# A sixth pair of k tiles by the 2x2 recurrence in the SwiGLU mixer, with three wide buffers for the weights' high parts served in turn

## Chip, core and metric

The kernel runs on one core of one Trainium2 chip. The metric is the device time of one execution in microseconds, lower is better. Every product is made in three passes on TensorE (high by high, high by low, low by high) from float32 values split into an fp32r high part and an fp32r rest.

## What is computed

Two layers over 256 positions of width 2048: a mixer (a gated recurrence beside a gated MLP in layer 0, windowed attention in layer 1), then in each layer the dense SwiGLU mixer, which the change touches:

```
def swiglu(h, w_in, w_out):
    g, u = jnp.split(h @ w_in, 2, axis=-1)        # w_in: 2048 x (2 x 5632)
    return (jax.nn.silu(g) * u) @ w_out           # w_out: 5632 x 2048
...
x = x + swiglu(rms_norm(x, ffn_norm[layer]), w_ffn_in[layer], w_ffn_out[layer])
```

## The kernel before

**Blocks and groups.** The 5632 hidden columns are cut into 11 blocks of 512. Block 0 goes through an older path of 16 chunks (lines 902 and 464 split their weights, line 1498 multiplies); each chunk counts up chunk_used. Blocks 1 to 10 go through groups, 12 a block and the same list each time: eight groups for the gate and up projections of block f (N_UP = 8, GROUPS_UP), then four down groups, D0 to D3, that multiply the hidden block f-1 into the four column groups of the output. A group is 1 MB of weights: 128 partitions by 4 slots of 512 columns. A group of kind plain holds one pair of k tiles and takes 24 matmuls, as a down group does. A group of kind strassen holds a pair of k tiles that is multiplied by a 2x2 scheme with seven products, 21 matmuls; it needs three sums of its slots (w_sum) and their high and low parts too. Before, a block is: plain 5, strassen 0, 1, 2, plain 6, strassen 3, 4, plain 7, D0, D1, D2, D3. Below, g0 to g11 are the places in this list (g8 to g11 are D0 to D3).

**Who does what for a group.** SP loads it into group_raw[g % 6] when the group six places earlier is used (line 353). VectorE, for a strassen group, makes three sums (sum_group: lines 1230, 1234, 1236). ScalarE casts the four slots to the high part group_hi[g % 4] (hi_group: line 708 for strassen, 715 else) and for strassen the three sums (line 711). VectorE subtracts to get the low parts (lo_group: line 1248, and 1253 for the sums). TensorE waits for group_lo_ready, multiplies (line 1714) and counts up group_used. Every engine takes its work strictly in the order in which its program lists it.

**Buffers of the high parts.** group_hi has four places, taken as g % 4: the cast of group g waits until group g-4 is used (free_group, line 699), and so does VectorE's second sum of a strassen group, which writes w_sum[g % 4] (line 1233). In a layer's first block the first four groups wait for chunks of block 0 instead (line 697): none for g0 and g3, 12 and 15 for g1 and g2.

**The results.** The gate and up sums of a block stand in eight banks of PSUM; out_sums and out_parts (lines 1268 to 1281) bring them together on VectorE after g9 and g10, silu and hidden (lines 677, 1167) make the hidden block, and turn_blocks (line 1177) with two DMAs on GpSimd's queue turns it, after which rows_hi and rows_lo (lines 683, 1183) split it. D0 and D2 write banks 0 and 1, D1 and D3 banks 2 and 3. ScalarE copies each out as y0 to y3 (copy_y, line 732), and GpSimd's queue adds it to x by a DMA (line 423). ScalarE's order in block f+1 for the four copies of block f is:

```
hi_(0)
if not first:
    copy_y(before, layer, 0)
    copy_y(before, layer, 1)
hi_(1)
if not first:
    copy_y(before, layer, 2)
hi_(2)
if not first:
    copy_y(before, layer, 3)
```

TensorE starts D2 of a block only when that block's y0 is copied and D3 when y1 is (line 1779), and g1 of the next block when y3 is (line 1772). In the last block the four copies stand after the block, with no cast of a following block ahead of the first.

**VectorE's order in a block** is g0 to g4, rows_lo, g5 to g9, out_sums, g10, out_parts, g11, hidden, turn_blocks; in the first block rows_lo comes after g5, and hidden and turn_blocks of block 0 stand between g1 and g2.

Of the kernel before, what the change touches and what calls it, by code (L numbers as in the profile page):

```python
# [20 lines left out]
F32R = mybir.dt.float32r  # L21
# [5 lines left out]
P = 128  # L27
# [4 lines left out]
W = 512  # L32
# [23 lines left out]
RING = 8  # L56
# [18 lines left out]


BLOCKS = FB - 1
GROUPS_UP = [("plain", 5), ("strassen", 0), ("strassen", 1), ("strassen", 2),
             ("plain", 6), ("strassen", 3), ("strassen", 4), ("plain", 7)]
N_UP = len(GROUPS_UP)  # L80
BLOCK_GROUPS = N_UP + GROUPS
LAST_STRASSEN = max(g for g, (kind, _) in enumerate(GROUPS_UP) if kind == "strassen")
HI_DONE = list(itertools.accumulate([2 if kind == "strassen" else 1 for kind, _ in GROUPS_UP] + [1] * GROUPS))
PAIRS = sum(kind == "strassen" for kind, _ in GROUPS_UP)
STRASSEN_BEFORE = [sum(kind == "strassen" for kind, _ in GROUPS_UP[:g]) for g in range(N_UP)]


# [18 lines left out]
def trunk(nc, x_in, final_norm, w_ab_in, a_lb_raw, b_v_norm, w_ab_out, w_qkv, c_sinks, w_c_out,  # L106
# [4 lines left out]
    with ctx:  # L111
# [9 lines left out]
        def sem(name):  # L121
# [14 lines left out]
        scratch = bias_at + 8 * KB  # L136
        place[0] = scratch + 76 * KB
        u_mid = sb("u_mid", [P, W])
        consts = sb("consts", [P, N_CONST, P])
        junk = sb("junk", [P, W])  # L140
        cols = sb("cols", [P, 80])
# [42 lines left out]
        gate = sb("gate", [P, NT, 1024], at=r1 + 36 * KB)  # L184
        end = r1 + 44 * KB

        group_hi = [sb("g0_hi", [P, 4, W], F32R, at=bias_at), sb("g1_hi", [P, 7, W], F32R, at=hi_at),
                    sb("g2_hi", [P, 7, W], F32R, at=hi_at + 14 * KB), sb("g3_hi", [P, 7, W], F32R, at=bias_at + 8 * KB)]
        raw_places = [raw_at, raw_at + 8 * KB] + [lo_at + 8 * KB * i for i in range(4)]
        group_raw = [sb(f"g{i}_raw", [P, 4, W], at=place_) for i, place_ in enumerate(raw_places)]  # L190
        group_lo = [sb(f"g{i}_lo", [P, 4, W], F32R, at=place_) for i, place_ in enumerate(raw_places)]
# [1 line left out]
        sum_lo = [None] + [sb(f"w{i}_lo", [P, 3, W], F32R, at=bias_at + (16 + 6 * i) * KB) for i in range(1, 4)]  # L193
        s_size = 512 * PAIRS
        s_hi = [sb(f"s{i}_hi", [P, PAIRS, P], F32R, at=bias_at + 40 * KB + i * s_size) for i in range(4)]
        s_lo = [sb(f"s{i}_lo", [P, PAIRS, P], F32R, at=bias_at + 50 * KB + i * s_size) for i in range(4)]
        s_sum = sb("s_sum", [P, 4, PAIRS, P], at=bias_at + 60 * KB)
        x_sum = sb("x_sum", [P, PAIRS, 2, T], at=bias_at + 22 * KB)
        gu = sb("gu", [P, 4, W], at=bias_at + 68 * KB)
# [258 lines left out]
        def _(act):  # L458
# [234 lines left out]

            def free_group(f, layer, g, first, base):

                if first and g < 4:
                    act.wait_ge(chunk_used, RING * base + (0, 12, 15, 0)[g])
                else:
                    act.wait_ge(group_used, f * BLOCK_GROUPS + (group_at(layer, 0) + g - 3))

            def hi_group(f, layer, g, first, base):

                free_group(f, layer, g, first, base)
                src, dst = group_raw[g % 6], group_hi[g % 4]
                if g < N_UP and GROUPS_UP[g][0] == "strassen":
                    n = 3 * (STRASSEN_BEFORE[g] - PAIRS)
                    act.wait_ge(sum_step, f * (3 * PAIRS) + (layer * BLOCKS * 3 * PAIRS + n + 1))
                    act.copy(dst[:, 0:4, :].rearrange("p s w -> p (s w)"),  # L708
                             src[:, :, :].rearrange("p s w -> p (s w)")).then_inc(group_hi_ready, 1)
                    act.wait_ge(sum_step, f * (3 * PAIRS) + (layer * BLOCKS * 3 * PAIRS + n + 3))  # L710
                    act.copy(dst[:, 4:7, :].rearrange("p s w -> p (s w)"),  # L711
                             w_sum[g % 4][:, :, :].rearrange("p s w -> p (s w)")).then_inc(group_hi_ready, 1)
                else:
                    act.wait_ge(pair_landed[g % 6], f * 64 + (32 * (group_at(layer, 0) // 6 + g // 6 + 1)))
                    act.copy(dst[:, 0:4, :].rearrange("p s w -> p (s w)"),  # L715
                             src[:, :, :].rearrange("p s w -> p (s w)")).then_inc(group_hi_ready, 1)
# [17 lines left out]
            def ffn(layer, base):  # L734

                root(2 * layer + 1)
                act.wait_ge(rstd_ready, 2 * layer + 2)
                ahead(base + 1, 2)
                for n, i in enumerate((0, 2, 1, 3)):
                    act.wait_ge(s_step, 5 * layer + n + 2)  # L740
                    act.copy(s_hi[i][:, :, :], s_sum[:, i, :, :]).then_inc(s_hi_ready, 1)
                ahead(base + 1, 5)
                silu(0, layer, base)
                ahead(base + 1, 7)

                def block(f, first):

                    def hi_(g):
                        hi_group(f, layer, g, first, base)

                    before = 0 if isinstance(f, int) and f == 2 else f - 2
# [10 lines that stand above are left out]
                    hi_(3)  # L762
                    hi_(4)
                    if not first:
                        rows_hi(f - 1, layer, hT[0][0])
                    hi_(5)
                    if first:
                        rows_hi(f - 1, layer, hT[0][0])
                    for g in range(6, 10):
                        hi_(g)  # L770
                    copy_p1(f, layer)
                    hi_(10)
                    hi_(11)
                    silu(f, layer, base)

                block(1, True)
                block(2, False)
                with act.Fori(3, FB - 1) as f:
                    block(f, False)
                block(FB - 1, False)  # L780
                copy_y(FB - 2, layer, 0)
                copy_y(FB - 2, layer, 1)
                last = base + FFN_ROUNDS - 1
                act.wait_ge(group_used, group_at(layer, FB - 1) + 10)
                his(last, 0, 3)
                copy_y(FB - 2, layer, 2)
                hT_his(FB - 1, layer, hT[1][0])
                act.wait_ge(group_used, group_at(layer, FB - 1) + 11)
                his(last, 3, 6)
                copy_y(FB - 2, layer, 3)  # L790
                done[0] = last * RING + 6
# [106 lines left out]
        def _(dve):  # L898
# [324 lines left out]

            def sum_group(f, layer, g, first):

                b, w = group_raw[g % 6], w_sum[g % 4]
                n = 3 * (STRASSEN_BEFORE[g] - PAIRS)
                step = f * (3 * PAIRS) + (layer * BLOCKS * 3 * PAIRS + n)
                dve.wait_ge(pair_landed[g % 6], f * 64 + (32 * (group_at(layer, 0) // 6 + g // 6 + 1)))
                dve.tensor_tensor(b[:, 1, :], b[:, 1, :], b[:, 0, :], ALU.subtract).then_inc(sum_step, 1)  # L1230
                dve.wait_ge(sum_step, step + 1)
                if not first or g >= 4:
                    dve.wait_ge(group_used, f * BLOCK_GROUPS + (group_at(layer, 0) + g - 3))
                dve.tensor_tensor(w[:, 0, :], b[:, 3, :], b[:, 1, :], ALU.subtract).then_inc(sum_step, 1)
                dve.wait_ge(sum_step, step + 2)
                dve.tensor_tensor(w[:, 1:3, :], b[:, 0:4:2, :], w[:, 0:1, :].broadcast_to([P, 2, W]),  # L1236
                                  ALU.subtract).then_inc(sum_step, 1)

            def lo_group(f, layer, g):

                src, hi_part, lo_part = group_raw[g % 6], group_hi[g % 4], group_lo[g % 6]
                strassen = g < N_UP and GROUPS_UP[g][0] == "strassen"
                ready = f * HI_DONE[-1] + ((layer * BLOCKS - 1) * HI_DONE[-1] + HI_DONE[g])
                dve.wait_ge(group_hi_ready, ready - 1 if strassen else ready)
# [5 lines left out]
                                        hi_part[:, 0:4, :].rearrange("p s w -> p (s w)"), ALU.subtract)  # L1250
                if strassen:
                    dve.wait_ge(group_hi_ready, ready)
                    ins = dve.tensor_tensor(sum_lo[g % 4][:, :, :].rearrange("p s w -> p (s w)"),  # L1253
                                            w_sum[g % 4][:, :, :].rearrange("p s w -> p (s w)"),
                                            hi_part[:, 4:7, :].rearrange("p s w -> p (s w)"), ALU.subtract)
                ins.then_inc(group_lo_ready, 1)

# [26 lines left out]
            def ffn(layer, base):  # L1284
# [6 lines left out]
                ahead(base + 1, 7)  # L1291
                group(1, layer, 0, True)
                group(1, layer, 1, True)
                hidden(0, layer, base)
                turn_blocks(0, layer)
                group(1, layer, 2, True)

                def block(f, first, last):
                    for g in range(3 if first else 0, 5):
# [190 lines left out]
        def _(pe):  # L1490
# [227 lines left out]

            def plain_group(g, first, last):

                hi_part, lo_part = group_hi[g % 4], group_lo[g % 6]
                for q in range(4):
                    k = 2 * GROUPS_UP[g][1] + q // 2
                    for t in range(NT):
# [5 lines left out]

            def strassen_group(g, first, last):

                hi_part, lo_part, sums_lo = group_hi[g % 4], group_lo[g % 6], sum_lo[g % 4]
                p = GROUPS_UP[g][1]
                t0, t1 = slice(0, P), slice(P, T)
                x_part = lambda k, ts: (xT_hi[:, k, ts], xT_lo[:, k, ts])
# [8 lines left out]

            def down_group(g):

                hi_part, lo_part = group_hi[g % 4], group_lo[g % 6]
                n = g - N_UP
                for k in range(4):  # L1750
                    for t in range(NT):
# [190 lines left out]
def group_at(layer, f):  # L1942

    return (layer * BLOCKS + f - 1) * BLOCK_GROUPS
# [38 lines left out]
```

## Time and profile before

| | us |
|---|---|
| median of 3 runs | 2034.26 (2033.28 to 2034.81) |
| the profiled execution | 2033.34 |
| its span | 2031.5 |

The grouped blocks run from about 458 to 1081 us in layer 0 and from about 1378 to 2001 us in layer 1, that is some 1245 us of the span. Engines: PE is TensorE's matmul, PEld its weight load, DVE VectorE, ACT ScalarE, POOL GpSimd, SP SyncE. A timeline's columns are start, duration, engine, line, operation and tiles, and in brackets the engine's idle time before the instruction and who ended it. Matmuls overlap, so their pace is read from start to start, not from their durations.

### The profile page before, as it was taken

The page shows a single profiled execution, that of the slowest core. Times are in us where ns is not written, and L with a number is a line of the kernel's source. Part 1 is how long each engine was busy: PE and PEld are TensorE (multiplying, and loading weights), DVE is VectorE, ACT ScalarE, POOL GpSimd, SP SyncE. Part 2 cuts the span into 40 slices and gives each one's busy share as a digit, 9 for nine tenths or more (in the row PEclk, how much of TensorE's full clock was granted, in tenths as well). Part 3 has the DMA queues.
Part 4 walks back from the last instruction along what each step waited for, and adds up shares of the span by engine and source line. Part 5 has one row for each costly group of instructions (what it writes and reads, how often), then busy time and mean ns, then how long its engine had stood idle before and what let it go on. Part 6 is the DMA issues. An engine that isn't in the chain of part 4 may idle for free.

```text
span 2031.5 us, 24678 instructions
## 1 busy us (share of the span) xinstructions
PE 2008.3 (99%) x9278; PEld 1666.2 (82%) x9278; DVE 1647.5 (81%) x1556; ACT 1179.9 (58%) x1195; POOL 170.6 (8%) x216
## 2 busy tenths in 40 slices
PE   8999999999999999999999999999999999999998
PEld 6888888887888888888888887787888888888886
DVE  5656777779999999999986467779999999999995
ACT  6745655555665555656556466555656556655554
POOL 0000000100111101111100000100111101111010
PEclk9999999999999999999999999999999999999999
DMA  7755443866998888988877644666988889988885
GB/s 262 228 177 166 159 151 131 275 208 209 269 256 253 243 248 261 268 248 256 244 244 228 190 145 145 218 222 222 269 248 251 246 248 268 267 251 238 249 261 160
DMA packets 237187, 461.40 MB, mean 227 GB/s; under 512 B 16480, under 2 KB 21376, under 8 KB 236992
## 3 DMA queue, kind: packets, MB, share of 16 engines
q1 hardware_dynamic: 202832, 386.97, 56.6%
q0 software_dynamic: 30496, 69.22, 16.8%
q10 hardware_dynamic: 3792, 4.34, 0.7%
q8 instruction: 39, 0.64, 0.1%
q14 instruction: 28, 0.23, 0.0%
HBM read 401.10 MB, written 17.29 MB: 206 GB/s over the span
## 4 chain that ended last, share of the span: by engine, by line
PE 92%; DVE 4%; ACT 2%; DMA 1%; issue 1%; ACTq 0%; SPq 0%; DVEq 0%
PE ps L1714 58%; PE ps L1498 30%; DVE g_lo L1248 1%; PE ps L1605 1%; DVE w_lo L902 1%; DMA raw<-in_w_ab_in 1%; DVE w_sum L1236 0%; DVE w_lo L1253 0%; PE ps L1524 0%; PE ps L1865 0%; ACT w_hi L464 0%; PE ps L1840 0%; ACT probs L830 0%; ACT junk L507 0%; DMA x<-in_x 0%
## 5 line engine op out<-in xcount | busy, mean ns | idle before, releaser
L1248 DVE TENSOR_TENSOR g_lo<-g_raw,g_hi 128x2048 fp32r<-128x2048 f32 x240 | 547.3, 2288 | 54.2 <-ACT g_hi L715 30.9
L902 DVE TENSOR_TENSOR w_lo<-raw,w_hi 128x1024 fp32r<-128x1024 f32 x248 | 294.4, 1220 | 153.8 <-ACT w_hi L464 145.4
L715 ACT CAST g_hi<-g_raw 128x2048 fp32r<-128x2048 f32 x140 | 265.5, 1911 | 156.1 <-PE ps L1714 150.4
L464 ACT ACTIVATE w_hi<-raw 128x1024 fp32r<-128x1024 f32 x248 | 254.0, 1056 | 140.2 <-DMA raw<-in_w_ab_in 50.1
L708 ACT CAST g_hi<-g_raw 128x2048 fp32r<-128x2048 f32 x100 | 191.5, 1915 | 221.0 <-DVE g_raw L1230 221.0
L1714 PE MATMUL ps<-g_hi,xT_hi 128*128 128x512 f32 x780 | 303.9, 390 | 5.0 <-DVE w_lo L1253 5.0
L1714 PE MATMUL ps<-g_hi,xT_lo 128*128 128x512 f32 x780 | 303.4, 389 | 0.0
L1498 PE MATMUL ps<-w_hi,xT_hi 128*128 128x512 f32 x672 | 265.3, 395 | 1.2 <-DVE xT_lo L921 1.1
L1714 PE MATMUL ps<-g_lo,xT_hi 128*128 128x512 f32 x680 | 264.6, 389 | 0.0
L1498 PE MATMUL ps<-w_hi,xT_lo 128*128 128x512 f32 x672 | 262.3, 390 | 0.0
L1498 PE MATMUL ps<-w_lo,xT_hi 128*128 128x512 f32 x672 | 262.1, 390 | 0.0
L1714 PE MATMUL ps<-g_hi,h0T_hi 128*128 128x512 f32 x640 | 249.1, 389 | 0.0
L1714 PE MATMUL ps<-g_hi,h0T_lo 128*128 128x512 f32 x640 | 249.0, 389 | 0.0
L1714 PE MATMUL ps<-g_lo,h0T_hi 128*128 128x512 f32 x640 | 249.0, 389 | 0.0
L423 POOL DMA_DIRECT2D x<-y x80 | 95.9, 1198 | 990.2 <-ACT y L732 704.2
L1714 PEld LDWEIGHTS ps<-g_hi,xT_hi 128*128 128x128 f32 x780 | 146.4, 188 | 37.0 <-DVE w_lo L1253 6.7
L1253 DVE TENSOR_TENSOR w_lo<-w_sum,g_hi 128x1536 fp32r<-128x1536 f32 x100 | 175.1, 1751 | 0.0
L1714 PEld LDWEIGHTS ps<-g_hi,xT_lo 128*128 128x128 f32 x780 | 146.4, 188 | 30.4
L1714 PE MATMUL ps<-g_hi,s_hi 128*128 128x512 f32 x400 | 155.7, 389 | 0.0
L1714 PE MATMUL ps<-g_hi,s_lo 128*128 128x512 f32 x400 | 155.6, 389 | 0.0
L711 ACT CAST g_hi<-w_sum 128x1536 fp32r<-128x1536 f32 x100 | 148.5, 1485 | 11.1 <-DVE w_sum L1236 10.1
L1498 PEld LDWEIGHTS ps<-w_hi,xT_hi 128*128 128x128 f32 x672 | 126.6, 188 | 28.5 <-DVE xT_lo L921 1.5
(222 smaller groups left out, 3041.1 us busy)
## 6 DMA issues: line engine op xcount, KB each, us to landing
g_raw<-in_w_ffn_in SPq DMA_DIRECT2D x320, 512.0 KB, 4.8
g_raw<-in_w_ffn_out SPq DMA_DIRECT2D x160, 512.0 KB, 4.7
raw<-in_w_ab_in SPq DMA_DIRECT2D x96, 512.0 KB, 4.8
x<-y POOLq DMA_DIRECT2D x80, 512.0 KB, 6.6
raw<-in_w_qkv SPq DMA_DIRECT2D x40, 512.0 KB, 4.5
raw<-in_w_ab_out SPq DMA_DIRECT2D x32, 512.0 KB, 4.7
raw<-in_w_ffn_in SPq DMA_DIRECT2D x32, 512.0 KB, 4.6
raw<-in_w_c_out SPq DMA_DIRECT2D x32, 512.0 KB, 5.2
```

Source lines behind the costliest of these rows:

```text
L423: pool.dma_start(x[:, :, n * W:(n + 1) * W], y[n % 2][:, :, :], accum_op=ALU.add).then_inc(y_landed[n % 2], 16)
L464: act.activation(w_hi[:, s, :], raw[:, s % RAWS, :], ACT.Copy).then_inc(hi_ready, 1)
L708: act.copy(dst[:, 0:4, :].rearrange("p s w -> p (s w)"), src[:, :, :].rearrange("p s w -> p (s w)")).then_inc(group_hi_ready, 1)
L711: act.copy(dst[:, 4:7, :].rearrange("p s w -> p (s w)"), w_sum[g % 4][:, :, :].rearrange("p s w -> p (s w)")).then_inc(group_hi_ready, 1)
L715: act.copy(dst[:, 0:4, :].rearrange("p s w -> p (s w)"), src[:, :, :].rearrange("p s w -> p (s w)")).then_inc(group_hi_ready, 1)
L902: dve.tensor_tensor(w_lo[:, s, :], raw[:, s % RAWS, :], w_hi[:, s, :], ALU.subtract).then_inc(lo_ready, 1)
L1248: ins = dve.tensor_tensor(lo_part[:, 0:4, :].rearrange("p s w -> p (s w)"), src[:, :, :].rearrange("p s w -> p (s w)"), hi_part[:, 0:4, :] ...
L1253: ins = dve.tensor_tensor(sum_lo[g % 4][:, :, :].rearrange("p s w -> p (s w)"), w_sum[g % 4][:, :, :].rearrange("p s w -> p (s w)"), hi_pa ...
L1498: ins = pe.matmul(banks[:, t, :], a[:, k0 + h, ts], w[:, s, h * W:(h + 1) * W], start=first and h == 0 and i == 0, stop=last and h == 1 an ...
L1605: ins = pe.matmul(side[t][:, c], E[:, t, c], E[:, t, c], start=True, stop=True)
L1714: ins = pe.matmul(bank, a, w, start=first and i == 0, stop=last and i == 2)
```

## The change

GROUPS_UP becomes plain 6, strassen 0 to 5, plain 7: k tiles 10 and 11, which were plain 5, are multiplied as the sixth strassen pair, and the six strassen groups g1 to g6 stand in a row. There are still 12 groups and 1 MB for each. The places of the high parts are taken from a list, HI_OF, in which place 0 (four slots, no room for sums) serves g7 and g10 and the three wide places 1, 2 and 3 serve the others. HI_BACK tells how many groups back the same place was used last: 3, 5, 3, 3, 3, 3, 3, 9, 4, 3, 3, 6 for g0 to g11, where it was 4 for all. The high places 1 and 2 exchange their addresses, s_lo moves partly over the masks in consts, and in the last block three casts wait for one group more. In a layer's first block the three sums of g2 stand ahead of hidden of block 0 on VectorE.

```
-GROUPS_UP = [("plain", 5), ("strassen", 0), ("strassen", 1), ("strassen", 2),
-             ("plain", 6), ("strassen", 3), ("strassen", 4), ("plain", 7)]
+GROUPS_UP = [("plain", 6)] + [("strassen", p) for p in range(6)] + [("plain", 7)]
...
+HI_OF = [2, 3, 1, 2, 3, 1, 2, 0, 3, 2, 0, 1]
+HI_BACK = [next(d for d in range(1, BLOCK_GROUPS + 1) if HI_OF[(g - d) % BLOCK_GROUPS] == h) for g, h in enumerate(HI_OF)]
...
-        group_hi = [sb("g0_hi", [P, 4, W], F32R, at=bias_at), sb("g1_hi", [P, 7, W], F32R, at=hi_at),
-                    sb("g2_hi", [P, 7, W], F32R, at=hi_at + 14 * KB), sb("g3_hi", [P, 7, W], F32R, at=bias_at + 8 * KB)]
+        group_hi = [sb("g0_hi", [P, 4, W], F32R, at=bias_at), sb("g1_hi", [P, 7, W], F32R, at=hi_at + 14 * KB),
+                    sb("g2_hi", [P, 7, W], F32R, at=hi_at), sb("g3_hi", [P, 7, W], F32R, at=bias_at + 8 * KB)]
...
-        s_lo = [sb(f"s{i}_lo", [P, PAIRS, P], F32R, at=bias_at + 50 * KB + i * s_size) for i in range(4)]
+        s_lo_at = [bias_at + 52 * KB, bias_at + 55 * KB, consts_at + 512, consts_at + 512 + s_size]
+        s_lo = [sb(f"s{i}_lo", [P, PAIRS, P], F32R, at=s_lo_at[i]) for i in range(4)]
...
             def free_group(f, layer, g, first, base):
-                if first and g < 4:
-                    act.wait_ge(chunk_used, RING * base + (0, 12, 15, 0)[g])
+                if first and g < HI_BACK[g]:
+                    act.wait_ge(chunk_used, RING * base + (0, 15, 12, 0)[HI_OF[g]])
                 else:
-                    act.wait_ge(group_used, f * BLOCK_GROUPS + (group_at(layer, 0) + g - 3))
+                    act.wait_ge(group_used, f * BLOCK_GROUPS + (group_at(layer, 0) + g + 1 - HI_BACK[g]))
             def hi_group(f, layer, g, first, base):
...
-                src, dst = group_raw[g % 6], group_hi[g % 4]
+                src, dst = group_raw[g % 6], group_hi[HI_OF[g]]
...
-                act.wait_ge(group_used, group_at(layer, FB - 1) + 11)
+                act.wait_ge(group_used, group_at(layer, FB - 1) + 12)
                 his(last, 3, 6)
...
             def sum_group(f, layer, g, first):
...
-                if not first or g >= 4:
-                    dve.wait_ge(group_used, f * BLOCK_GROUPS + (group_at(layer, 0) + g - 3))
+                if not first or g >= HI_BACK[g]:
+                    dve.wait_ge(group_used, f * BLOCK_GROUPS + (group_at(layer, 0) + g + 1 - HI_BACK[g]))
...
                 group(1, layer, 0, True)
                 group(1, layer, 1, True)
+                sum_group(1, layer, 2, True)
                 hidden(0, layer, base)
                 turn_blocks(0, layer)
-                group(1, layer, 2, True)
+                lo_group(1, layer, 2)
```

## Rows read from the trace of the kernel before

**Rows 1.** The page: span, and busy time of each engine.
```profile
span 2031.5 us, 24678 instructions
PE 2008.3 (99%) x9278; PEld 1666.2 (82%) x9278; DVE 1647.5 (81%) x1556; ACT 1179.9 (58%) x1195; POOL 170.6 (8%) x216
```
**Rows 2.** TensorE's waits over the span: us in total, times, longest.
```profile
PE ps L1714 <- DVE w_lo L1253: 5.0, 4, 1.4
```
**Rows 3.** Windows: a middle block (D3's end to the next), then layer 0's first block.
```profile
832.90:894.80 61.90, 61.90 (x274) 51.26 (x273) 56.73 (x43) 36.53 (x26) 7.62 (x9) 1.00 0.85 255
458.40:523.50 65.10, 62.56 (x275) 51.17 (x274) 62.43 (x50) 38.29 (x26) 7.48 (x11) 1.00 0.72 225
```
**Rows 4.** VectorE's waits within the middle block, 832.9 to 894.8 us.
```profile
DVE g_lo L1248 <- ACT g_hi L715: 1.2, 1, 1.2
DVE u_mid L1268 <- ACT gu L722: 1.1, 1, 1.1
```
**Rows 5.** Timeline of TensorE: a stall of the first block, then D3's last matmul.
```profile
489.43 0.39 PE L1714 MATMUL ps<-g_hi,s_lo 128*128 128x512 f32 x1
491.20 0.50 PE L1714 MATMUL ps<-g_hi,xT_hi 128*128 128x512 f32 x1 [1.38 <-DVE w_lo L1253]
491.54 0.39 PE L1714 MATMUL ps<-g_lo,xT_hi 128*128 128x512 f32 x1
...
832.48 0.39 PE L1714 MATMUL ps<-g_hi,h0T_lo 128*128 128x512 f32 x1
832.71 0.39 PE L1714 MATMUL ps<-g_hi,xT_hi 128*128 128x512 f32 x1
```
**Rows 6.** Timeline of VectorE in a middle block, g1 to g5.
```profile
824.98 2.29 DVE L1248 TENSOR_TENSOR g_lo<-g_raw,g_hi 128x2048 fp32r<-128x2048 f32 x1 [0.99 <-ACT g_hi L708]
...
835.63 0.68 DVE L1230 TENSOR_TENSOR g_raw<-g_raw 128x512 f32<-128x512 f32 x1
...
838.42 2.29 DVE L1248 TENSOR_TENSOR g_lo<-g_raw,g_hi 128x2048 fp32r<-128x2048 f32 x1
...
842.30 2.28 DVE L1248 TENSOR_TENSOR g_lo<-g_raw,g_hi 128x2048 fp32r<-128x2048 f32 x1
844.50 1.22 DVE L1183 TENSOR_TENSOR h0T_lo<-hid_rows,h0T_hi 128x1024 fp32r<-128x1024 f32 x1
845.64 0.68 DVE L1230 TENSOR_TENSOR g_raw<-g_raw 128x512 f32<-128x512 f32 x1
```
**Rows 7.** Timeline of ScalarE at the start of a middle block: cast of g0, then y0, y1, y3.
```profile
816.66 1.91 ACT L715 CAST g_hi<-g_raw 128x2048 fp32r<-128x2048 f32 x1 [2.36 <-PE ps L1714]
818.48 1.00 ACT L732 COPY y<-ps 128x1024 f32<-128x1024 f32 x1
822.03 1.02 ACT L732 COPY y<-ps 128x1024 f32<-128x1024 f32 x1 [2.54 <-PE ps L1714]
...
833.77 1.02 ACT L732 COPY y<-ps 128x1024 f32<-128x1024 f32 x1 [0.54 <-DMA x<-y]
```
**Rows 8.** Timelines of ScalarE and of VectorE at layer 0's entry into the first block.
```profile
444.74 1.91 ACT L715 CAST g_hi<-g_raw 128x2048 fp32r<-128x2048 f32 x1 [3.05 <-DMA g_raw<-in_w_ffn_in]
...
446.68 2.29 DVE L1248 TENSOR_TENSOR g_lo<-g_raw,g_hi 128x2048 fp32r<-128x2048 f32 x1 [3.74 <-ACT g_hi L715]
...
458.48 1.41 DVE L1167 SCALAR_TENSOR_TENSOR hid<-ps,rstd,hid 128x512 f32<-128x512 f32 x2 [2.86 <-PE ps L1498]
...
463.89 2.29 DVE L1248 TENSOR_TENSOR g_lo<-g_raw,g_hi 128x2048 fp32r<-128x2048 f32 x1
```
**Rows 9.** Timeline of GpSimd's queue: the DMA that adds y1.
```profile
824.99 1.18 POOL L423 DMA_DIRECT2D x<-y  x1 [3.35 <-issue]
```
**Rows 10.** Timeline of TensorE's first wait and of early matmuls.
```profile
7.08 1.94 PE L1524 MATMUL ps<-consts,x 128*128 128x128 f32 x8 [7.08 <-DMA x<-in_x]
...
12.37 0.63 PE L1498 MATMUL ps<-w_hi,xT_lo 128*128 128x512 f32 x1
12.80 0.63 PE L1498 MATMUL ps<-w_hi,xT_hi 128*128 128x512 f32 x1
```

More of the change, by code:

```diff
@@ L138, in trunk @@
         u_mid = sb("u_mid", [P, W])
+        consts_at = place[0]
         consts = sb("consts", [P, N_CONST, P])
@@ L711, in hi_group @@
                     act.copy(dst[:, 4:7, :].rearrange("p s w -> p (s w)"),
-                             w_sum[g % 4][:, :, :].rearrange("p s w -> p (s w)")).then_inc(group_hi_ready, 1)
+                             w_sum[HI_OF[g]][:, :, :].rearrange("p s w -> p (s w)")).then_inc(group_hi_ready, 1)
                 else:
@@ L1224, in sum_group @@
             def sum_group(f, layer, g, first):
-                b, w = group_raw[g % 6], w_sum[g % 4]
+                b, w = group_raw[g % 6], w_sum[HI_OF[g]]
                 n = 3 * (STRASSEN_BEFORE[g] - PAIRS)
@@ L1239, in lo_group @@
             def lo_group(f, layer, g):
-                src, hi_part, lo_part = group_raw[g % 6], group_hi[g % 4], group_lo[g % 6]
+                src, hi_part, lo_part = group_raw[g % 6], group_hi[HI_OF[g]], group_lo[g % 6]
                 strassen = g < N_UP and GROUPS_UP[g][0] == "strassen"
@@ L1252, in lo_group @@
                     dve.wait_ge(group_hi_ready, ready)
-                    ins = dve.tensor_tensor(sum_lo[g % 4][:, :, :].rearrange("p s w -> p (s w)"),
-                                            w_sum[g % 4][:, :, :].rearrange("p s w -> p (s w)"),
+                    ins = dve.tensor_tensor(sum_lo[HI_OF[g]][:, :, :].rearrange("p s w -> p (s w)"),
+                                            w_sum[HI_OF[g]][:, :, :].rearrange("p s w -> p (s w)"),
                                             hi_part[:, 4:7, :].rearrange("p s w -> p (s w)"), ALU.subtract)
@@ L1719, in plain_group @@
             def plain_group(g, first, last):
-                hi_part, lo_part = group_hi[g % 4], group_lo[g % 6]
+                hi_part, lo_part = group_hi[HI_OF[g]], group_lo[g % 6]
                 for q in range(4):
@@ L1731, in strassen_group @@
             def strassen_group(g, first, last):
-                hi_part, lo_part, sums_lo = group_hi[g % 4], group_lo[g % 6], sum_lo[g % 4]
+                hi_part, lo_part, sums_lo = group_hi[HI_OF[g]], group_lo[g % 6], sum_lo[HI_OF[g]]
                 p = GROUPS_UP[g][1]
@@ L1746, in down_group @@
             def down_group(g):
-                hi_part, lo_part = group_hi[g % 4], group_lo[g % 6]
+                hi_part, lo_part = group_hi[HI_OF[g]], group_lo[g % 6]
                 n = g - N_UP
```

## The prediction

> **What bounds the kernel now.** I read the page first. TensorE is busy 2008.3 of 2031.5 us [rows 1], and over the whole span it waited for VectorE in the groups four times, 5.0 us in all [rows 2]. So TensorE sets the time. But busy shares are an average, and the change works in the grouped blocks alone, so the windows come next [rows 3]: a middle block takes 61.9 us, all of it TensorE's, and VectorE is busy 56.73 us of it, far more than its 81% of the page. In a layer's first block TensorE already has 2.5 us idle (65.10 less 62.56). The reader is to see that there are two engines near the bound.
>
> TensorE's pace: two neighbouring matmuls start at 832.48 and 832.71, 0.23 us apart [rows 5]; to another digit, a middle block has 273 matmuls (3 plain x 24, 5 strassen x 21, 4 down x 24) in 61.9 us, 0.2267 us each. So a strassen group is 4.76 us, any other 5.44.
>
> VectorE's pace, from start to start [rows 6]: a strassen group 835.63 to 842.30, 6.67 us; a plain or down group 842.30 to 844.50, 2.20; rows_lo 844.50 to 845.64, 1.14. The sums of a strassen group are 2.79 of its 6.67 (835.63 to 838.42).
>
> **The sum if only TensorE counted.** One pair turns from 24 to 21 matmuls in 20 blocks: 60 x 0.2267 = 13.6 us less. The block would be 61.2 us.
>
> **VectorE.** A group of 2.20 us becomes one of 6.67, so 4.47 us more a block. How much room is there? Of the 61.9 us it waits 1.2 and 1.1 us [rows 4] and 0.52 and 0.99 at g1; of these the 0.99 is for ScalarE's cast and not for TensorE [rows 6]. Its work with the small gaps between instructions is thus 61.9 - 3.8 = 58.1 us; with 4.47 it is 62.6, and 63.6 if the 0.99 stays. That is above 61.2. But it is an average as well, and the order in the block matters more: six strassen groups in a row take VectorE 6 x 6.67 = 40.0 us and TensorE 28.6, so VectorE loses 11.4 us of lead there (before: runs of three and two). How much lead it can have is set by when a place of high parts comes free.
>
> **The chain through D3.** g2 now takes a place last used by g11, that is D3, three back. So VectorE's second sum of g2 can't start before D3 is used, as a sum of g1 is held now. Call the start of g0's first matmul after D3 zero. An engine released by a group's end starts 0.2 us after that point (D3 ends at 832.71, two groups of 5.44 earlier D1 ended, 821.83, and y1 started at 822.03) [rows 5, 7]. From there: g2 needs two sums and its low parts, 6.67 less the first sum's 0.8, which is done already: it is ready for TensorE at 6.1. g3 and g4 at 12.8 and 19.4, rows_lo 20.6, g5 27.2, g6 33.9. Do the casts hold it longer? Their places are free in time: g3's at 5.44, g4's at 10.2, g5's at 15.0, each before VectorE comes to it. TensorE would like to start g6 at 5.44 + 5 x 4.76 = 29.2. It waits first at g5 (2.7 us behind, and 2.0 more at g6), and g6 starts at 33.9 + 0.06 wake-up. A matmul after a stall has its successor 0.34 us later and not 0.23 (491.20, 491.54), 0.11 more [rows 5]. g6 starts 4.8 us later than TensorE could. Then g6, g7 and the downs: 4.76 + 5 x 5.44 = 32.0.
>
> **The copy of y0.** g0 took the place of D0 before (four back, g8); now it takes that of D1 (three back, g9). ScalarE's order is hi_(0), then y0. Before, the cast of g0 started 0.27 us after D0's end (816.66 against 832.71 - 3 x 5.44 = 816.39), y0 started at 818.48 and was copied at 819.48, while TensorE was still in D1 until 821.83: hidden [rows 5, 7]. Now the same cast starts 0.27 us after D1's end, and D2 needs y0 copied. So TensorE stands between D1 and D2 for 0.27 + 1.82 + 1.02 + 0.06 = 3.17 us, with the 0.11 after a stall 3.28. Nothing covers it: D2 is next in TensorE's order. This happens in nine blocks of a layer (in the tenth no cast stands ahead of y0): 18 x 3.28 = 59 us.
>
> **A middle block then:** 33.9 + 0.17 + 32.0 + 3.28 = 69.4 us against 61.9, 7.5 more. Eight of them a layer: 60.0.
>
> **The last block** has the chain and no wait for y0: 66.1 against 61.9, 4.2 more (what else it does is as before). Its casts of three chunks wait for all 12 groups instead of 11; three chunks of TensorE, 12 x 0.2267 = 2.7 us each, stand before they are used, 8.2 us for a cast and a subtraction of some 2.3: nothing. y3 is copied behind these casts, some 3 us later, and is needed by TensorE only after four chunks, 10.9 us: nothing.
>
> **The first block.** The high part of g0 sits in place 2, and waits for 12 chunks of the block before. The 16th ends at 458.48 as VectorE sees it, so the 12th at 458.48 - 4 x 2.72 = 447.6, while g0's cast started at 444.74 before [rows 8]. VectorE starts g0 at 447.6 + 1.94 = 449.5 (was 446.68), has g0 and g1 at 458.4, the moved sums of g2 at 461.2, and hidden and turn_blocks (458.48 to the sums of g2, where the rest of 463.89 - 458.48 = 5.4 less 2.74 is 2.7) at 463.9. The low part of g2 starts at 463.9, where it started before: the moved sums give 2.7 us and the late g0 takes them. Hidden is done at 462.6, before TensorE ends g0 at 463.7. Then g3, g4, g5 by 6.67, rows_lo, g6: 463.9 + 3.9 + 20.0 + 1.1 + 6.7 = 495.6, so TensorE starts g6 at 495.7 where it was 491.20 [rows 5, 8]. With the wait for y0: 4.6 + 3.3 = 7.9 us more.
>
> **Small things.** The sums of the positions before block 0 grow by a fifth; VectorE waits 3.74 us ahead of g0 there [rows 8] and more now, so I take 0, with 2 us a layer as the bound if they delay a chunk instead. Loads: 1 MB a group as before, six places, and the block is longer: 0, and a DMA share of 0.85 [rows 3] that falls. GpSimd's queue: y1 was copied at 823.05, its DMA issued at 824.99, and y3's copy waited for it until 833.77, 10.7 us after the copy [rows 7, 9]. y1 is now copied about 10.1 us before zero, so y3 can go at 0.6, while ScalarE comes to it at 3.6 (behind the two casts of g2), ready at 4.6, before g1 at 5.44: 0. Should it be later, up to 2.7 us of it vanish in the wait at g5.
>
> **Sum.** A layer: 7.9 + 60.0 + 4.2 = 72.1, two layers 144. The profiled execution took 2033.3, so 2177.5, and 0.9 us of difference to the median shown gives 2178. I forecast 2178 us, 7.1% slower.
>
> **The rivals.**
> *TensorE's work decides* (faster, 2020.7 us). For it: TensorE waits 5 us in all. It holds if VectorE's work stays under 61.2 us and y0 is copied in time. The point where it decides is 61.2 - 58.1 = 3.1 us of added work, and the work added is 4.47. 3 in 100.
> *VectorE decides, but only by its total*: 63.6 a block, 1.7 x 20 = 34, the first blocks' g6 some 3 us more each beyond that: 2074 us. It needs places that come free early enough, against the threes of HI_BACK. 3 in 100.
> *No wait for y0*, as where the copy were issued ahead of the cast; the chain through D3 alone: 2178 - 59 = 2119 us. The order of ScalarE's program speaks against it. 3 in 100.
> *The chain through D3 is covered*, since the sums of g2 to g6 find slack that I missed; y0's wait alone: 2034 - 13.6 + 59 + 10.6 for g6 of the two first blocks (4.6 late and 0.7 not saved, each) = 2090 us. Against it: the chain has only work of VectorE itself in it, at the pace of rows 6. 3 in 100.
> *TensorE's clock falls in the stalls.* The granted clock is 1.00 in both windows of rows 3, over the stall of 1.38 us too, where the next matmuls came at 0.23 again. Only at the start, after 7.08 us without work, the pace was 0.43 (12.37 to 12.80) [rows 10], the lower of the two levels; some eight matmuls ran so, from 10.07 us on, 1.6 us lost. After each stall of 3.2 us that would be 18 x 1.6 = 29 us: 2207; with those at g5 and g6 in part, up to 2235. Against it: the stall is half of the one at the start, and TensorE is full before it. 9 in 100. The Trainium skill has a rule that speaks for this rival: TensorE: Matmul & The Clock Gate, section "Why this matters for your kernels", asks to avoid idle gaps of TensorE between bursts of matmuls, or the clock falls back to half. By that rule the result would be nearer 2207 us than 2178; no stall as long as these is in the middle of this trace.
> *A DMA is late too*: y1's landing behind the rows of the hidden block, some 1 to 2 us a block, 2195 to 2215. For it: y3 waited 0.54 us for it already [rows 7]. Against: the 2.7 us at g5 that swallow it. 3 in 100.
>
> The forecast has 76 in 100. Its own uncertainty is half a microsecond a block in either direction, 2166 to 2190. The four cases below it hold 12 in 100 and lie far off, so the range goes down only to 2155, room for slack of a microsecond a block that I have not seen; above it takes in the clock's first price and most of the late DMA, 2212, and leaves out the clock's higher ones. A change under 0.2% is about what a measurement of this kernel can't tell from none. Faster 0.03, within 0.2% 0.01, slower 0.96.
>
> **What would show it.** The window of a middle block: 69.4 us, TensorE busy about 61 to 62, VectorE about 61. TensorE's waits: y (ScalarE, line 732) 18 times, near 3 us each; w_lo some 4 to 5 us a block, at g5 and g6. ScalarE's y0 no longer idle before D1's end. VectorE's second sum of g2 waiting for TensorE, some 2 us. ScalarE's cast of g0 in the first block at 447.6, and TensorE's start of g6 near 495.7. The granted clock 1.00 throughout. The forecast is wrong if D2 follows D1 without a gap, if VectorE is not waiting ahead of g2, or if the clock of the blocks is below 1.

## The result and the profile after

The changed kernel takes 2204.01 us (2202.75 to 2205.66, 4 runs) against 2034.1 us: a ratio of 1.0837, 95% interval 1.0823 to 1.0851, 170 us slower. The forecast was 2178 us in a range of 2155 to 2212.

The page of the changed kernel, its first lines, the granted clock by slices, and the chain by engine:

```profile
span 2203.9 us, 24482 instructions
PE 2054.6 (93%) x9218; PEld 1677.8 (76%) x9218; DVE 1735.0 (79%) x1636; ACT 1211.5 (55%) x1215; POOL 170.5 (8%) x216
...
PEclk9999999999999999999999999999999999999999
...
PE 62%; DVE 26%; issue 6%; ACT 4%; DMA 1%; ACTq 0%; DVEq 0%; SPq 0%
```

Against [rows 1], TensorE has its 60 matmuls less (9218), and it is idle for 149.3 us of the span where it was idle for 23.2. That is 126 us more; the other 46 us are busy time, slower matmuls among it. The two largest of its waits over the span, where [rows 2] had 5.0 us:

```profile
PE ps L1718 <- DVE w_lo L1256: 76.1, 34, 2.8
PE ps L1718 <- ACT y L735: 54.5, 18, 3.1
```

Both are the waits that were forecast: y0 in 18 blocks, and the row of strassen groups. Two middle blocks, D3's end to the next (start:end, length, busy time and count of PE, PEld, DVE, ACT, POOL, then the granted clock, DMA share, GB/s), to hold against the first of [rows 3]:

```profile
534.50:604.20 69.70, 62.19 (x272) 50.40 (x271) 60.91 (x46) 38.06 (x26) 7.11 (x8) 1.00 0.77 225
604.20:675.50 71.30, 65.47 (x271) 52.69 (x271) 60.91 (x47) 38.03 (x26) 8.18 (x10) 0.95 0.79 225
```

The first is the forecast block, 69.7 us where 69.4 was worked out. The second does the same work and has 1.6 us more, with a granted clock of 0.95. What lies between them is seen on TensorE ahead of D2, first without and then with a slower clock (timeline: start, duration, then the idle time and who ended it):

```profile
593.00 0.49 PE L1718 MATMUL ps<-g_hi,h0T_hi 128*128 128x512 f32 x1 [3.06 <-ACT y L735]
593.33 0.39 PE L1718 MATMUL ps<-g_lo,h0T_hi 128*128 128x512 f32 x1
593.57 0.40 PE L1718 MATMUL ps<-g_hi,h0T_lo 128*128 128x512 f32 x1
...
662.70 0.53 PE L1718 MATMUL ps<-g_hi,h0T_hi 128*128 128x512 f32 x1 [3.05 <-ACT y L735]
663.03 0.63 PE L1718 MATMUL ps<-g_lo,h0T_hi 128*128 128x512 f32 x1
663.45 0.63 PE L1718 MATMUL ps<-g_hi,h0T_lo 128*128 128x512 f32 x1
...
666.01 0.59 PE L1718 MATMUL ps<-g_hi,h0T_lo 128*128 128x512 f32 x1
666.44 0.39 PE L1718 MATMUL ps<-g_hi,h0T_hi 128*128 128x512 f32 x1
```

The wait is the same, 3.06 and 3.05 us. After the second wait the matmuls from 663.03 on come 0.43 us apart, at the lower of the two levels (1.2 GHz), until 666.44, and eight of them lose 8 x 0.2 = 1.6 us. Of the eighteen waits for y0, thirteen were followed by such a stretch: the blocks from D3 to D3 take 71.2 to 71.3 us where it is so and 69.5 to 69.7 where it is not.

ScalarE and VectorE of the changed kernel between two D3s, to be held against [rows 6, 7]:

```profile
590.07 1.90 ACT L718 CAST g_hi<-g_raw 128x2048 fp32r<-128x2048 f32 x1 [4.21 <-PE ps L1718]
591.87 1.92 ACT L735 COPY y<-ps 128x1024 f32<-128x1024 f32 x2
```
```profile
600.89 0.68 DVE L1233 TENSOR_TENSOR g_raw<-g_raw 128x512 f32<-128x512 f32 x1
604.21 0.69 DVE L1237 TENSOR_TENSOR w_sum<-g_raw 128x512 f32<-128x512 f32 x1 [2.64 <-PE ps L1718]
...
610.20 0.68 DVE L1233 TENSOR_TENSOR g_raw<-g_raw 128x512 f32<-128x512 f32 x1
...
616.87 0.69 DVE L1233 TENSOR_TENSOR g_raw<-g_raw 128x512 f32<-128x512 f32 x1
...
636.42 1.75 DVE L1256 TENSOR_TENSOR w_lo<-w_sum,g_hi 128x1536 fp32r<-128x1536 f32 x1
```

The cast of g0 starts at D1's end, the two copies follow it with no idle time, and TensorE starts D2 at 593.00. VectorE stands for 2.64 us ahead of the second sum of g2, until D3 is used, and then goes through the row at 6.67 us a group until g6 is ready at 638.2, 34.0 us later. Where a slow stretch stands ahead of D3, VectorE waits 4.2 to 4.4 us there.

### The profile page after: what moved, and what is told of

The parts are those of the page before. It is cut to its first block, busy times and chain, and to the rows that moved or that the text cites. A ratio compares the mean times of both kernels' runs of the same rounds, so it can differ in the third digit from the quotient of the medians.

```text
span 2203.9 us, 24482 instructions
## 1 busy us (share of the span) xinstructions
PE 2054.6 (93%) x9218; PEld 1677.8 (76%) x9218; DVE 1735.0 (79%) x1636; ACT 1211.5 (55%) x1215; POOL 170.5 (8%) x216
## 4 chain that ended last, share of the span: by engine, by line
PE 62%; DVE 26%; issue 6%; ACT 4%; DMA 1%; ACTq 0%; DVEq 0%; SPq 0%
PE ps L1718 32%; PE ps L1502 25%; DVE g_lo L1251 8%; DVE w_lo L1256 6%; DVE w_sum L1239 4%; DVE w_sum L1237 3%; DVE g_raw L1233 2%; ACT g_hi L711 1%; DVE h0T_lo L1186 1%; PE ps L1609 1%; ACT y L735 1%; DVE w_lo L905 1%; ACT w_hi L467 1%; DMA raw<-in_w_ab_in 0%; DMA raw<-in_w_ffn_out 0%
## 5 line engine op out<-in xcount | busy, mean ns | idle before, releaser
L1718 PE MATMUL ps<-g_hi,xT_hi 128*128 128x512 f32 x680 | 272.0, 400 | 76.4 <-DVE w_lo L1256 76.1
L1718 PE MATMUL ps<-g_hi,h0T_hi 128*128 128x512 f32 x640 | 259.6, 406 | 54.5 <-ACT y L735 54.5
L1718 PE MATMUL ps<-g_hi,xT_lo 128*128 128x512 f32 x680 | 265.7, 391 | 0.0
L1718 PEld LDWEIGHTS ps<-g_hi,xT_hi 128*128 128x128 f32 x680 | 128.7, 189 | 123.3 <-DVE w_lo L1256 98.7
L1718 PE MATMUL ps<-g_lo,xT_hi 128*128 128x512 f32 x560 | 219.1, 391 | 0.0
L1256 DVE TENSOR_TENSOR w_lo<-w_sum,g_hi 128x1536 fp32r<-128x1536 f32 x120 | 210.2, 1752 | 0.0
L1718 PE MATMUL ps<-g_hi,s_hi 128*128 128x512 f32 x480 | 194.0, 404 | 0.0
L1718 PE MATMUL ps<-g_hi,s_lo 128*128 128x512 f32 x480 | 193.1, 402 | 0.0
L1718 PEld LDWEIGHTS ps<-g_hi,h0T_hi 128*128 128x128 f32 x640 | 125.0, 195 | 88.3 <-issue 55.3
L714 ACT CAST g_hi<-w_sum 128x1536 fp32r<-128x1536 f32 x120 | 178.1, 1484 | 13.5 <-DVE w_sum L1239 11.5
L1239 DVE TENSOR_TENSOR w_sum<-g_raw,w_sum 128x1024 f32<-128x1024 f32 x120 | 147.1, 1226 | 4.1
```

The source lines that it names most:

```text
L714: act.copy(dst[:, 4:7, :].rearrange("p s w -> p (s w)"), w_sum[HI_OF[g]][:, :, :].rearrange("p s w -> p (s w)")).then_inc(group_hi_ready, 1)
L1256: ins = dve.tensor_tensor(sum_lo[HI_OF[g]][:, :, :].rearrange("p s w -> p (s w)"), w_sum[HI_OF[g]][:, :, :].rearrange("p s w -> p (s w)"), ...
L1718: ins = pe.matmul(bank, a, w, start=first and i == 0, stop=last and i == 2)
```

## The experiments

All times in us. The ratio is to the kernel before, measured again beside each (2033.55 us for the first four, 2033.7 for the others), with its 95% interval.

| kernel | median | ratio |
|---|---|---|
| y0_first | 2139.61 | 1.0521 (1.0503 to 1.0538) |
| before_late_g0 | 2123.85 | 1.0442 (1.0424 to 1.0459) |
| filler | 2186.02 | 1.0749 (1.0731 to 1.0766) |
| interleaved | 2065.48 | 1.0156 (1.0139 to 1.0173) |
| before_sums | 2028.81 | 0.9976 (0.9966 to 0.9986) |
| sums_late | 2203.52 | 1.0835 (1.0819 to 1.0852) |
| extra_row | 2250.0 | 1.1064 (1.1047 to 1.1081) |
| extra_down | 2204.55 | 1.0838 (1.0821 to 1.0855) |

### The wait for y0, taken away from the changed kernel

```
-                    hi_(0)
                     if not first:
                         copy_y(before, layer, 0)
+                    hi_(0)
+                    if not first:
                         copy_y(before, layer, 1)
```

> The changed kernel, with ScalarE's copy of y0 ahead of the cast of the next block's g0. Theory: the cast of g0 waits for D1 and y0 stood behind it, so TensorE waited 3.1 us ahead of D2 in 18 blocks; without it a block without a clock fall goes from 69.65 to some 66.4 us, and the clock falls that follow that wait (13 of 1.6 us) go too: 2204 - 59 - 21 = 2124 us, 2112 to 2136. Rival: VectorE's work alone sets the block and the wait for y0 is only time in which it catches up: the wait for y0 goes but the waits for w_lo grow by as much, 2185 to 2205 us.

Measured: 2139.61 us, 64 less than the changed kernel, and no wait for y0 is left. So the order of one cast and one copy was worth about two fifths of the loss. The rival falls: the waits for w_lo stay at 76 us. The expected window was missed by 4 us. A block takes 67.0 us and not 66.4:

```profile
531.00:598.00 67.00, 63.86 (x271) 51.55 (x271) 60.82 (x47) 37.97 (x26) 6.84 (x9) 0.97 0.80 236
```
```profile
DVE g_lo L1252 <- ACT g_hi L718: 4.7, 3, 2.7
```

VectorE's waits in this block (second fence) have no wait for TensorE ahead of g2 any more, only waits for the casts of plain and down groups: with 3.3 us less between D1 and D3, D3 is used before VectorE comes to g2. The chain enters one step earlier, at D1, through the cast of g0: 0.27 + 1.91 for the cast, 2.2 for g0's low part, 6 x 6.67, 1.14 for rows_lo, 0.17, 4.76 for g6, and 3 x 5.44 for g7, D0 and D1 make 66.8. The slower clock (0.97 here) comes in the waits at g5, where TensorE has to wait for g6 anyway, and costs nothing in most blocks.

### The wait for y0, put into the kernel before

```
-                    act.wait_ge(group_used, f * BLOCK_GROUPS + (group_at(layer, 0) + g - 3))
+                    act.wait_ge(group_used, f * BLOCK_GROUPS + (group_at(layer, 0) + g - 3 + (g == 0)))
```

> The kernel before, with the cast of g0 made to wait for one group more (D1 instead of D0), nothing else. Theory: y0 stands behind that cast and TensorE waits some 3.2 us ahead of D2 in 18 blocks, 59 us, with up to 1.6 us more where the clock falls after it: 2093 us without a fall, 2114 with thirteen. VectorE has slack there and adds no wait of its own. Rival: the wait is hidden, since VectorE's slack of 3.8 us a block gives back what TensorE loses: under 2050 us.

Measured: 2123.85 us, 90 more than before, and above the 2114 us of thirteen falls. TensorE's waits are 54.5 us for y in 18 blocks, as in the changed kernel, and 5.1 us for VectorE, as before. One block with a slower clock, and one without it:

```profile
528.10:594.90 66.80, 63.74 (x274) 52.27 (x273) 56.97 (x43) 36.69 (x25) 7.66 (x9) 0.97 0.80 234
...
1493.70:1558.90 65.20, 62.15 (x274) 51.16 (x273) 55.15 (x43) 35.74 (x25) 7.08 (x8) 1.00 0.79 237
```

65.2 is 61.9 + 3.3: the wait at full price, 18 x 3.3 = 60 us. The other 30 us go with the clock. Of the sixteen middle blocks only this one has 65.2; the others take 66.5 to 66.9, and four of them 68.0, where the slower stretch was twice as long. So a wait of 3 us that costs 60 us by itself cost 90.

### TensorE kept busy in the wait for y0

```
+                        if g == N_UP + 2 and not last:
+                            pe.wait_ge(out_step, f * 5 + 5 * layer * BLOCKS)
+                            for _ in range(FILL):      # 12
+                                pe.matmul(P2, xT_hi[:, 0, 0:P], xT_hi[:, 0:2, :].rearrange("p k t -> p (k t)"), start=True, stop=True)
```

> The changed kernel, with twelve matmuls without use between D1 and D2, into a bank that is free there, 2.7 us, inside the 3.1 us wait for y0. Theory: the blocks of 71.2 us are those of 69.65 with a clock fall after the wait for y0; a busy TensorE keeps the clock at 1.00 there, and all middle blocks take 69.7 us: 2204 - 13 x 1.6 = 2183 us, 2178 to 2190. Rival: the 1.6 us come from a late DMA or from VectorE and the fall is only beside it: 2200 to 2210 us.

Measured: 2186.02 us, 18 less, for 216 matmuls more that nobody reads. TensorE's twelve fillers and D2 behind them:

```profile
588.47 2.88 PE L1786 MATMUL ps<-xT_hi 128*128 128x512 f32 x12
591.69 0.49 PE L1719 MATMUL ps<-g_hi,h0T_hi 128*128 128x512 f32 x1 [0.34 <-ACT y L736]
592.02 0.39 PE L1719 MATMUL ps<-g_lo,h0T_hi 128*128 128x512 f32 x1
```

All middle blocks take 69.5 to 69.7 us but two, with 70.6, where the slow stretch at g5 was twice as long. The wait itself is as long as it was; what went is the slow stretch after it. The rival, that a DMA or VectorE made the blocks of 71.2 us, falls. The clock still falls in this kernel, at g5, where it costs nothing in the other blocks, since TensorE waits for g6 all the same.

### Six strassen groups in another order, with places four back

```
-GROUPS_UP = [("plain", 6)] + [("strassen", p) for p in range(6)] + [("plain", 7)]
+GROUPS_UP = [("plain", 6), ("strassen", 0), ("strassen", 1), ("strassen", 2),
+             ("plain", 7), ("strassen", 3), ("strassen", 4), ("strassen", 5)]
-HI_OF = [2, 3, 1, 2, 3, 1, 2, 0, 3, 2, 0, 1]
+HI_OF = [g % 4 for g in range(BLOCK_GROUPS)]
```

The addresses of places 1 and 2 and the last block's wait are those of the kernel before, and the marks that close an accumulation follow the last group.

> Six pairs by the recurrence as in the change, but in the order plain, three strassen, plain, three strassen, four down groups, and the places g % 4 as in the kernel before (four groups back for all). Theory: the loss of the change is in the row of six with places only three back and in y0; with four back VectorE's total work decides, 63.4 us a block and no wait for y0: 2034 + 28 to 36 = 2062 to 2072 us. Rival A: VectorE's total is no limit and TensorE's 60 matmuls fewer show, 2020 to 2025. Rival B: six strassen groups cost VectorE as much in any order, 2110 us or more.

Measured: 2065.48 us.

```profile
525.40:588.90 63.50, 61.79 (x271) 50.40 (x271) 60.60 (x47) 37.94 (x27) 7.70 (x9) 1.00 0.87 248
```

The same work as in the changed kernel, VectorE busy 60.6 us and TensorE's matmuls the same, takes 63.5 us a block and not 69.7, with the clock at 1.00. So of the change's 170 us, some 138 are its order and its places together, the clock that falls in their waits included, and 32 are left. The times of rivals A and B both fall.

The time is in the expected window, but the 32 us are not shown to be VectorE's added work, as I had expected. VectorE waits once in each of the 20 blocks, and TensorE in each of the 16 middle ones (waits over the span: us in total, times, longest):

```profile
DVE u_mid L1272 <- ACT gu L726: 28.1, 20, 1.5
```
```profile
PE ps L1719 <- DVE u_mid L1272: 24.1, 16, 1.6
```

In this order a strassen group stands directly ahead of D0. ScalarE copies a sum of the block (gu) when that last strassen group is used, VectorE's out_sums (u_mid) needs the copy, and D0 needs out_sums. In the kernel before, VectorE waits there for 1.1 us too [rows 4], but plain 7 stands between and TensorE does not wait. Without its wait of 1.4 us, VectorE's work with the gaps between instructions is 63.5 - 1.4 = 62.1 us, hardly more than the 61.9 of the block before. So most of the 32 us can be this wait, which the new order brings, and how much VectorE's added work costs by itself was not tried.

### More work for VectorE, in the row and outside it

```
                 lo_group(f, layer, g)
+                if g == EXTRA_AT:      # 4 in extra_row, 8 in extra_down
+                    dve.tensor_reduce(far[:, 0, 0:6], xT_hi[:, 0:6, :], AX.X, ALU.add)
```

> The changed kernel with one more VectorE instruction a block, a reduction of 128x1536 values into a scratch that nobody reads, some 1.7 us, behind g4, in the row of strassen groups. Theory: the chain from D3 through g2 to g6 sets the block, and each us put into it lengthens the block by a us: 69.65 to 71.3, 20 blocks, 34 us more: 2232 to 2244 us. Rival: VectorE has 8 us of waits in a block and takes it from there: 2204 to 2210 us.

> The same added VectorE instruction of some 1.7 us, but behind g8, where VectorE then waits 2.7 us for the cast of g9. Theory (the chain): it is hidden, the block stays at 69.65, 2200 to 2208 us. Rival (VectorE's total work sets the block, wherever it stands): 34 us more, 2232 to 2244 us.

The added instruction takes the same time in both, 20 of them and 35 us in all:

```profile
L1270 DVE TENSOR_REDUCE far<-xT_hi 128x6 f32<-128x1536 f32 x20 | 34.9, 1746 | 0.0
```

Behind g8 it costs nothing: 2204.55 us, and blocks without a slower clock take 69.6 us. Behind g4 it costs 46 us: 2250.0 us. The two blocks (extra_row, then extra_down):

```profile
534.80:607.60 72.80, 65.21 (x272) 52.68 (x271) 62.58 (x47) 38.04 (x26) 7.67 (x9) 0.95 0.75 217
```
```profile
534.20:603.80 69.60, 62.09 (x271) 50.32 (x270) 62.58 (x47) 38.08 (x26) 7.12 (x8) 1.00 0.76 225
```

VectorE is busy 62.6 us in both, and one block is 3.2 us longer. So what counts is not VectorE's total but what stands in the chain from D3 through g2 to g6. It cost more than the expected 34 us, and more than the 2244 us of the window: of the 46 us, 33 are 20 x 1.66. The other 13 are read from the trace and were not tried: with a longer wait at g5 (4.4 us where it was 2.8) TensorE's matmuls ran slower after 17 of the 18 waits for y0, not after 13, and after nearly all waits at g5, which lasts into g6. The shortest middle block has 72.5 us: 69.6 + 1.7, and 1.2 for six slow matmuls after its wait for y0.

### The moved sums, alone and taken back

```
+                sum_group(1, layer, 2, True)
                 hidden(0, layer, base)
                 turn_blocks(0, layer)
-                group(1, layer, 2, True)
+                lo_group(1, layer, 2)
```

before_sums is the kernel before with this alone, sums_late the changed kernel without it.

> The kernel before, with one part of the change alone: in a layer's first block the sums of g2 stand ahead of hidden of block 0. There VectorE has an idle stretch of 2.9 us ahead of hidden. Theory: the sums fill it, g2 to g6 are ready 2.7 us earlier, and TensorE's two waits of the first block (2.5 us idle, 2.9 by starts) go: 2 x 2.9 = 5 to 6 us less, 2028 to 2029 us. Rival: hidden comes later by what the sums take and TensorE's wait only moves to g1: 2032 to 2035 us.

> The changed kernel with the sums of g2 put back behind hidden and turn_blocks. Theory: in the changed kernel the cast of g0 waits for chunk 12 and VectorE comes to hidden with no idle stretch left, so the order gives nothing: g6 of the first blocks starts at the same time within 0.3 us, 2200 to 2208 us (the clock falls vary by some us). Rival: the move is worth its 2.7 us a layer here as well: g6 later by 2.7 us in both first blocks, 2207 to 2212 us.

In the kernel before the move takes both waits of layer 0's first block away, and leaves 0.5 us of those in layer 1. TensorE comes to the groups of layer 0 at 458.28 us in the trace of before and at 459.86 in this one, so the first blocks are compared from there. Here are both layers of the kernel before, then both of before_sums:

```profile
458.28:523.30 65.02, 62.48 (x274) 51.10 (x273) 62.23 (x50) 38.09 (x26) 7.48 (x11) 1.00 0.71 224
1377.90:1443.00 65.10, 62.59 (x275) 51.10 (x274) 62.53 (x50) 38.41 (x26) 7.50 (x11) 1.00 0.72 223
```
```profile
459.86:522.10 62.24, 62.17 (x274) 51.17 (x273) 59.64 (x47) 35.85 (x25) 7.48 (x11) 1.00 0.76 233
1376.70:1439.40 62.70, 62.22 (x275) 51.18 (x274) 60.58 (x48) 37.24 (x26) 7.50 (x11) 1.00 0.75 233
```

That is 2.8 us less in layer 0 and 2.4 in layer 1, 5.2 in all, near the expected 2 x 2.9. The median is 2028.81 us, 4.9 us less than before, with an interval of the ratio that does not reach 1 (0.9966 to 0.9986). This is the fastest version here, and it is the one part of the change that pays. In the changed kernel it gives next to nothing: without it 2203.52 us against 2204.01, each with executions some us apart. TensorE starts g6 of layer 0's first block at 496.58 without it:

```profile
496.58 0.50 PE L1717 MATMUL ps<-g_hi,xT_hi 128*128 128x512 f32 x1 [2.73 <-DVE w_lo L1256]
```

and at 495.88 with it (below). Of these 0.7 us, 0.43 come from ahead of the block, where TensorE came to the groups at 459.21 without it and at 458.77 with it. The move itself is worth 0.27 us in this layer, and in layer 1 too (g6 37.38 us and 37.11 us after the first matmul of the groups). That is the 0.3 I expected, and not 2.7.

## Why the prediction was right

**The direction and the range held.** The three parts of the sum did as worked out, and a fourth, that I had as a rival, came on top.

**The chain through D3.** Forecast 69.4 us a middle block, measured 69.5 to 69.7 where the clock stayed up. VectorE waited 2.64 us for D3 ahead of g2, where "some 2 us" was said, and 4.2 to 4.4 us after a slow stretch. g5 and g6 are where TensorE waits. That it is a chain and no total is shown by extra_row against extra_down, and that it comes of order and places by interleaved.

**The copy of y0.** Forecast 3.28 us in 18 blocks; measured 3.3 (TensorE's starts 589.56 and 593.00, less one pace of 0.23, with 0.10 more to the next matmul), in 18 blocks. It is shown by taking it away (y0_first) and by putting it where it was not (before_late_g0).

**TensorE alone** would have given 13.6 us back. Its matmuls were fewer, but those left out were in the row g1 to g6, at whose end TensorE waits for VectorE.

**The first block.** The cast of g0 started at 448.09 (forecast 447.6), VectorE's first group at 450.04 (449.5), and TensorE's g6 at 495.88 (495.7). TensorE came to the groups 0.5 us later than in the trace of before (458.77, not 458.28); counted from there, the cast and VectorE's first group came as forecast, and g6 0.3 us earlier:

```profile
448.09 1.91 ACT L718 CAST g_hi<-g_raw 128x2048 fp32r<-128x2048 f32 x1 [4.28 <-PE ps L1502]
```
```profile
474.78 0.50 PE L1718 MATMUL ps<-g_hi,xT_hi 128*128 128x512 f32 x1 [0.89 <-DVE w_lo L1256]
481.44 0.50 PE L1718 MATMUL ps<-g_hi,xT_hi 128*128 128x512 f32 x1 [1.60 <-DVE w_lo L1256]
488.09 0.50 PE L1718 MATMUL ps<-g_hi,xT_hi 128*128 128x512 f32 x1 [1.60 <-DVE w_lo L1256]
495.88 0.79 PE L1718 MATMUL ps<-g_hi,xT_hi 128*128 128x512 f32 x1 [2.69 <-DVE w_lo L1256]
```

That the late g0 eats what the moved sums give holds to within 0.3 us a layer, as before_sums and sums_late show.

**What was mis-sized: the clock.** The likeliest case was 2178 us with its own range of 2166 to 2190, and the time is above it. The time lies in the stated range because that was drawn to take in the clock's first price, not because the likeliest case came true: "the clock of the blocks is below 1" was one of the prediction's own signs of being wrong, and it is 0.95 to 0.98 in eleven of the sixteen middle blocks. The step is the rival "TensorE's clock falls in the stalls", to which I gave 9 in 100 because the 3.2 us are half of the only wait after which the trace of before showed the slow pace, and because a wait of 1.38 us showed none. Between these two there was no row, and I read the gap in my favour. The Trainium skill's rule that was cited beside it (TensorE: Matmul & The Clock Gate, "Why this matters for your kernels") spoke for the fall, and the traces agree with it, in thirteen waits of eighteen. The price for one, 1.6 us, was right: 18 x 1.6 gave 2207.

**The account.** The spans differ by 2203.9 - 2031.5 = 172.4 us. The forecast had 144. Thirteen slow stretches after y0 and one after g6 of each first block (the matmul of 0.79 us above, and the first block of layer 1 likewise) are 15 x 1.6 = 24; the middle blocks are 0.25 us longer than worked out, 16 x 0.25 = 4. That makes 172. Two smaller differences cancel: the first blocks together are 1.1 us shorter than worked out, and the span outside the groups is 1.1 us longer. The 13 stretches are shown by filler. For the first block of layer 0 a second execution serves: sums_late had no slow stretch in it, the changed kernel had both (after g6 and after y0). The changed kernel, then sums_late:

```profile
458.80:534.40 75.60, 65.92 (x272) 52.61 (x271) 64.20 (x52) 37.11 (x25) 8.03 (x12) 0.95 0.64 196
```
```profile
459.20:531.90 72.70, 62.76 (x272) 50.30 (x271) 64.40 (x52) 37.16 (x25) 7.48 (x11) 1.00 0.64 202
```

The 2.9 us between them are 2 x 1.6 less the 0.3 of the moved sums.

**What stays open.** Why some waits for y0 are followed by the lower clock and others of the same length are not was not tried. A version in which six pairs pay was not found. The nearest is interleaved, at 63.5 us a block against 61.9, with 1.4 us in which VectorE waits ahead of out_sums; an order with places four back and a plain group last, as before, was not tried, so it is open whether VectorE's 62.1 us or TensorE's work would then set the block.

## What to carry to other kernels

Count an engine's work along the order of the program and between two releases, not over the whole block: VectorE had 4 us of waits in a block of 62 and the change added 4.5, yet the block grew by 7.8 us, and by 5.1 with the wait for y0 taken away (y0_first), since a row of heavy groups needs a lead that the places of the buffers did not allow. And a new order can bring a new wait of its own, as interleaved did ahead of D0. When a buffer comes free one step later, look at what stands behind the waiting instruction in its engine's order: here it was not the cast that mattered but a copy of 1 us behind it. And a new wait of TensorE of about 3 us must be priced with the slower clock after it.

## What the runs showed of the hardware

Waits of TensorE of 3.05 and 3.06 us, with the same work before them, were followed by a granted clock at the lower level in one case and at the full one in the other, 13 times of 18 in the changed kernel and in all but one of the sixteen middle blocks of before_late_g0. Waits of 1.5 us, one in each middle block of interleaved, were followed by none (granted clock 0.999 over the span). The slow stretch costs 1.6 us in the changed kernel and 1.3 to 1.7 in before_late_g0, and where it was twice as long 2.8 (68.0 us against 65.2). Keeping TensorE busy with matmuls without use through such a wait gave 18 us back.
